# The joint of a convolution and its output projection, run by token block

## What is computed

```python
def conformer_conv(x, w_in, b_in, dw, dw_b, ln_g, ln_b, w_out, b_out):
    h = x @ w_in + b_in
    a, gate = jnp.split(h, 2, axis=-1)
    h = a * jax.nn.sigmoid(gate)
    h = causal_dwconv(h, dw, dw_b)            # 31 taps, per channel
    h = jax.nn.silu(layer_norm(h, ln_g, ln_b))
    return h @ w_out + b_out
```

## Time and profile before

| | us |
|---|---|
| median of three runs | 2142.02 |
| lowest and highest | 2141.66, 2143.29 |
| span of the profiled execution | 2140.8 |
| TensorE busy in it | 2125.7 (99%) |
| VectorE, ACT busy | 1452.6 (68%), 1056.8 (49%) |
| all DMA | 399 MB, mean 186 GB/s |

### The profile page before, as it was taken

One profiled execution on the slowest core, in us unless ns is written; L12 is line 12 of the kernel. 1 busy time (PEld: TensorE's weight loads), 2 busy tenths in 40 slices (PEclk: granted clock), 3 DMA queues, 4 the chain that ended last, 5 costly groups with the idle time before them and its releaser, 6 DMA issues.

```text
span 2140.8 us, 30475 instructions
## 1 busy us (share of the span) xinstructions
PE 2125.7 (99%) x11011; PEld 1812.3 (85%) x11011; DVE 1452.6 (68%) x2137; ACT 1056.8 (49%) x1501; POOL 45.7 (2%) x50
## 2 busy tenths in 40 slices
PE   9999999999999999999999999999999999999998
PEld 7788788888888888888888888888888888888887
DVE  6766757777777774454688867667777777764444
ACT  7554655544445443444554444554544445444443
POOL 5300000000000000000000000000000000000000
PEclk9999999999999999999999999999999999999999
DMA  8555456666666655555656554566666666656553
GB/s 309 175 186 191 138 178 183 190 191 183 194 184 189 191 185 189 193 190 191 191 163 176 181 175 155 191 182 183 190 190 184 194 183 189 192 190 215 195 195 114
DMA packets 513820, 399.07 MB, mean 186 GB/s; under 512 B 6558, under 2 KB 425848, under 8 KB 513408
## 3 DMA queue, kind: packets, MB, share of 16 engines
q1 hardware_dynamic: 513568, 397.96, 60.0%
q10 hardware_dynamic: 192, 0.28, 0.0%
HBM read 396.11 MB, written 2.10 MB: 186 GB/s over the span
## 4 chain that ended last, share of the span: by engine, by line
PE 95%; DVE 2%; DMA 1%; ACT 1%; SPq 0%; issue 0%; DVEq 0%; ACTq 0%
PE acc L1520 35%; PE acc L1525 18%; PE acc L1554 12%; PE acc L1555 12%; PE acc L1556 12%; PE acc L1826 1%; PE acc L1825 1%; PE acc L1824 1%; DMA sb_stage<-in_conv_w_in 1%; DVE sb_w_lo L918 1%; PE aux L1595 0%; PE aux L1835 0%; ACT sb_w_hi L564 0%; PE aux L1783 0%; PE aux L1664 0%
## 5 line engine op out<-in xcount | busy, mean ns | idle before, releaser
L918 DVE TENSOR_TENSOR sb_w_lo<-sb_stage,sb_w_hi 128x1024 fp32r<-128x1024 f32 (+1 forms) x743 | 904.9, 1221 | 516.8 <-ACT sb_w_hi L564 513.4
L564 ACT ACTIVATE sb_w_hi<-sb_stage 128x1024 fp32r<-128x1024 f32 (+1 forms) x743 | 780.4, 1053 | 657.4 <-PE acc L1556 373.9
L1520 PE MATMUL acc<-sb_normed,sb_w_hi 128*128 128x512 f32 x3264 | 1027.6, 396 | 0.0
L1525 PEld LDWEIGHTS acc<-sb_normed,sb_w_lo 128*128 128x128 f32 x3264 | 613.2, 188 | 144.8
L1525 PE MATMUL acc<-sb_normed,sb_w_lo 128*128 128x256 f32 x3264 | 641.4, 278 | 0.0
L1520 PEld LDWEIGHTS acc<-sb_normed,sb_w_hi 128*128 128x128 f32 x3264 | 497.7, 189 | 0.6
L1554 PE MATMUL acc<-sb_w_hi,sb_hidden 128*128 128x512 f32 x674 | 262.5, 389 | 0.0
L1556 PE MATMUL acc<-sb_w_hi,sb_hidden 128*128 128x512 f32 x674 | 262.3, 389 | 0.0
L1555 PE MATMUL acc<-sb_w_lo,sb_hidden 128*128 128x512 f32 x674 | 262.3, 389 | 0.0
L576 ACT ACTIVATE sb_corr<-acc 128x256 f32<-128x256 f32 x204 | 76.8, 376 | 210.8 <-PE acc L1525 210.7
L1556 PEld LDWEIGHTS acc<-sb_w_hi,sb_hidden 128*128 128x128 f32 x674 | 126.5, 188 | 26.4
(11 more groups left out here) (221 smaller groups left out, 1645.1 us busy)
## 6 DMA issues: line engine op xcount, KB each, us to landing
sb_stage<-in_ffn_w_gate SPq DMA_DIRECT2D x86, 1024.0 KB, 5.4
sb_stage<-in_ffn_w_up SPq DMA_DIRECT2D x86, 1024.0 KB, 5.5
sb_stage<-in_ffn_w_down SPq DMA_DIRECT2D x80, 1024.0 KB, 5.0
sb_stage<-in_attn_w_qkv SPq DMA_DIRECT2D x48, 1024.0 KB, 5.3
sb_stage<-in_conv_w_in SPq DMA_DIRECT2D x30, 1024.0 KB, 5.6
sb_stage<-in_conv_w_out SPq DMA_DIRECT2D x16, 1024.0 KB, 5.1
sb_stage<-in_attn_w_o SPq DMA_DIRECT2D x16, 1024.0 KB, 5.0
sb_stage<-in_ffn_w_down SPq DMA_DIRECT2D x8, 768.0 KB, 4.4
```

The costliest lines, as they stand in the source:

```text
L564: nc.scalar.activation(w_hi[:, (2 * first + h) % PIECES, 0:size], stage[:, first % STAGES, off:off + size], ACT.Copy).then_inc(hi_ready, 1)
L918: nc.vector.tensor_tensor(w_lo[:, slot, 0:size], stage[:, first % STAGES, off:off + size], w_hi[:, slot, 0:size].bitcast(F32), ALU.subtrac ...
L1520: nc.tensor.matmul(acc[:, bank, :], w_hi[:, slot, q * P:(q + 1) * P], operand[:, k, :], start=begin, stop=False, skip_group_check=True)
L1525: return nc.tensor.matmul(acc[:, bank, T:2 * T], w_lo[:, slot, q * P:(q + 1) * P], operand[:, k, 0:T], start=False, stop=end, skip_group_c ...
```

## The change

- The two token halves no longer go through the joint together. Statistics, root, scaling, transposes, SiLU and splits of the first four channel tiles are done for the first 128 tokens, then for the other 128 (`ln_moments`, `ln_sqrt`, `ln_invert`, `ln_scale`, `turn_first`, `first_quarter`, `first_split`). TensorE's order is written out in `open_project`: first half through two weight blocks with the second half's inverse and transposes set in between, then the second half through the same two blocks.
- `glu`, `multiply`, `prod_hi`, `prod_lo`, `forward` and `inverse` can be called for one half or one part, and ACT's and VectorE's queues at the joint are set in a new order. The SiLU and root tables are loaded twice each. The dummies are gone.
- The high and low parts of the second `conv_out` block move in both queues; the bias additions come two blocks later.
- In all four chunks `prev_op` is no longer written by ACT and VectorE. `load_prev` on SP copies it with three DMAs out of `glu_op`, the split operand of the first half. For the first three chunks they are issued behind the load of blocks 14, 22 and 30, for the last behind the fifth load of `conv_out`.

The core of the diff:

```diff
+            def load_prev(c):
+                if c:
+                    sp.wait_ge(forward_done, 4 * c)
+                sp.wait_ge(glu_split, TB * c + 1)
+                for at, part in ((0, 0), (32, 1), (64, 0)):
+                    sp.dma_start(prev_op[at:at + 32, :].bitcast(F32), glu_op[P - 32:P, 0, part, :].bitcast(F32)).then_inc(prev_loaded, 16)
...
                     load_in_rows(c)
+                if at % 8 == 6:
+                    load_prev(at // 8 - 1)
             load_dw_bias(CH - 1)
 
             def load_bias():
 
+                load_prev(CH - 1)
                 sp.wait_ge(pieces_done, 2 * B["conv_out"])
...
-                act.wait_ge(glu_ready, TB * c + 1)
-                for at in (0, 64):
-                    nc.scalar.activation(prev_op[at:at + 32, :], value_t[0][P - 32:P, :], ACT.Copy).then_inc(prev_high, 1)
...
-            glu_hi(last)
+            glu_hi(last, [0])
+            for h in range(2):
+                hi(0, (0, B["conv_out"] + 1), h)
+            glu_hi(last, [1])
+            prod_hi(last, 0, [0])
             keep_conv(last - 1, 0, acc)
-            prod_hi(last, 0)
+            prod_hi(last, 0, [1])
             keep_conv(last - 1, 1, acc)
-            prod_hi(last, 1)
-            keep_conv(last, 0, acc, TB)
-            hi(0, (0, B["conv_out"] + 1), 0)
             warm_up(ACT.Sqrt)
...
+            ln_sqrt(0)
+            first_quarter(0, lambda: prod_hi(last, 1, [1]))
+            keep_conv(last, 0, acc, TB)
+            warm_up(ACT.Sqrt)
+            ln_sqrt(1)
+            first_quarter(1)
             keep_conv(last, 1, acc, TB)
-            hi(0, (0, B["conv_out"] + 1), 1)
...
-                if b:
-                    nc.vector.tensor_tensor(prev_op[32:64, :], value_t[0][P - 32:P, :],
-                                            glu_op[P - 32:P, 0, 0, :].bitcast(F32), ALU.subtract).then_inc(prev_split, 1)
...
+            multiply(last, 0, [0])
+            glu_lo(last, 1)
+            multiply(last, 0, [1])
+            prod_lo(last, 0)
+            measure_conv(last - 1, 0)
+            multiply(last, 1, [0])
+            measure_conv(last, 0)
+            ln_moments(0)
+            multiply(last, 1, [1])
+            ln_invert(0)
+            ln_scale(0, 0, 2)
+            prod_lo(last, 1, [0])
+            ln_scale(0, 2, 2)
+            first_split(0, 0)
+            prod_lo(last, 1, [1])
+            for k in range(1, BANKS):
+                first_split(0, k)
+            measure_conv(last - 1, 1)
+            for h in range(2):
+                lo(0, (0, B["conv_out"] + 1), h)
+            measure_conv(last, 1)
+            ln_moments(1)
+            ln_invert(1)
+            ln_scale(1, 0, 2)
+            ln_scale(1, 2, 2)
+            own.done()
+            for k in range(BANKS):
+                first_split(1, k)
...
                     if b:
-                        pe.wait_ge(prev_high, 2 * c + 2)
-                        pe.wait_ge(prev_split, c + 1)
+                        pe.wait_ge(prev_loaded, 48 * (c + 1))
...
-            forward(CH - 1, [0])
-            inverse(CH - 2, acc)
-            forward(CH - 1, [1])
-            inverse(CH - 1, acc, TB)
-            keep_clock(aux[:, 3, 0:P], 9)
+            last = CH - 1
+            forward(last, [0])
+            inverse(last - 1, acc)
+            forward(last, [1], [0])
+            inverse(last, acc, TB, [0])
+            forward(last, [1], [1])
...
+            def open_project():
+                for b in range(TB):
+                    for at in range(2):
+                        c, n = ORDER["conv_out"][at][0], B["conv_out"] + at
+                        bank = (C["conv_out"] + TB * c + b) % BANKS
+                        pe.wait_ge(conv_kept, TB * (CH - 2) + TB * at + b + 1)
+                        for k in range(KB):
+                            h, q = divmod(k, KB // 2)
+                            slot, wide = (2 * n + h) % PIECES, slice(WIDE * q, WIDE * (q + 1))
+                            if (b, at, k) == (0, 0, 2):
+                                inverse(last, acc, TB, [1])
+                            elif (b, at, k) == (0, 1, 1):
+                                turn_first(1)
+                            elif (b, at, k) == (1, 1, 1):
+                                turn_norm(1)
...
+                            if b == TB - 1 and q == 1:
+                                ins.then_inc(pieces_done, 1)
```

More of the change, by code:

```diff
@@ L617, in open_gate, with glu_hi @@
                     nc.scalar.activation(gate_t[b], gate_t[b], ACT.Sigmoid).then_inc(gate_opened, 1)
-            def glu_hi(c):
-                for b in range(TB):
+            def glu_hi(c, rows=range(TB)):
+                for b in rows:
                     act.wait_ge(glu_ready, TB * c + b + 1)
@@ L636, in prod_hi @@
                         act.wait_ge(inverse_done, TB * c)
-                for m in range(2):
+                for m in parts:
                     act.wait_ge(prod_ready, 4 * c + 2 * b + m + 1)
@@ L995, in keep_gate, with glu_value @@
                                                    op1=ALU.add).then_inc(evacuated, 1)
[L997 to L1010, removed]
-                    nc.vector.tensor_tensor(value_t[b], value_t[b], gate_t[b], ALU.mult).then_inc(glu_ready, 1)
-                    if b or c == CH - 1:
-                        glu_lo(c, b)
+            def glu_value(c, b):
+                if c == CH - 1 and b == 0:
+                    dve.wait_ge(rows_done, 1)
+                else:
+                    dve.wait_ge(pieces_done, 2 * (8 * c + 8))
+                nc.vector.scalar_tensor_tensor(out=value_t[b], in0=acc[:, TB + b, :], scalar=row_scale[:, 0, b:b + 1],
+                                               in1=in_rows[:, c % 2, 1, :], op0=ALU.mult,
+                                               op1=ALU.add).then_inc(evacuated, 1)
@@ L1021, in glu_lo, with glu, multiply @@
                 nc.vector.tensor_tensor(glu_op[:, b, 1, :], value_t[b], glu_op[:, b, 0, :].bitcast(F32),
                                         ALU.subtract).then_inc(glu_split, 1)
-            def multiply(c, b):
-                for m in range(2):
+            def glu(c):
+                glu_value(c, 0)
+                glu_gate(c, 0)
+                glu_value(c, 1)
+                glu_lo(c, 0)
+                glu_gate(c, 1)
+                glu_lo(c, 1)
+            def multiply(c, b, parts=range(2)):
+                for m in parts:
@@ L1033, in multiply, with prod_lo @@
                                             ALU.mult).then_inc(prod_ready, 1)
-            def prod_lo(c, b):
-                for m in range(2):
+            def prod_lo(c, b, parts=range(2)):
+                for m in parts:
                     dve.wait_ge(prod_high, 4 * c + 2 * b + m + 1)
@@ L1167, in _ @@
-            own.done()
+            last = CH - 1
+            glu_value(last, 0)
+            glu_gate(last, 0)
+            glu_lo(last, 0)
+            glu_value(last, 1)
+            glu_gate(last, 1)
+            multiply(last, 0, [0])
[7 more added lines that the diff above has]
+            multiply(last, 1, [1])
@@ L1169, in norm_quarter @@
+            ln_scale(1, 2, 2)
+            own.done()
+            for k in range(BANKS):
+                first_split(1, k)
+            for b in range(TB):
+                ln_scale(b, 4, 4)
             def norm_quarter(q):
@@ L1597, in turn_resid, with project @@
                     ins.then_inc(resid_turned, 1)
-            def project(name, operand, tiles, arrivals, between=None, turn=True):
+            def project(name, operand, tiles, arrivals, between=None, turn=True, begin=0):
                 for at, (c, j) in enumerate(ORDER[name]):
+                    if at < begin:
+                        continue
                     before = ENDS[name].get(at - 1) if turn else None
@@ L1666, in triple, with forward @@
                 return nc.tensor.matmul(out, s_lo, m_hi, start=False, stop=end)
-            def forward(c, rows=range(TB)):
+            def forward(c, rows=range(TB), parts=range(2)):
                 if c == 0:
@@ L1685, in forward, with inverse @@
                                (glu_op[:, b, 0, :], glu_op[:, b, 1, :]), b == 0, True).then_inc(forward_done, 1)
-            def inverse(c, banks, at_bank=0):
-                for b in range(TB):
+            def inverse(c, banks, at_bank=0, rows=range(TB)):
+                for b in rows:
                     for m in range(2):
@@ L1756, in up @@
+            turn_first(0)
+            open_project()
+            project("conv_out", conv_op, KD, [(k, OPER["norm"] + BANKS + k + 1) for k in range(BANKS, KD)], next_norm, begin=2)
             def up(name, before):
```

137 lines of the change are left out of this document (76 added, 61 removed).

## The result

The changed kernel takes 2158.39 us (median of 4, 2157.83 to 2160.19) beside 2141.84 us (2141.30 to 2143.29) for the kernel before on the same chip: a ratio of 1.0077, 95% interval 1.0065 to 1.0089, so some 16.5 us slower. The profiled execution spans 2156.3 us, 15.4 more than the 2140.8 of before. It took 2158.07 us, so 1.8 us lie around its span (1.8 to 2.0 in the other runs that show both). By that the profiled execution of before took some 2142.6 us, an estimate, which is above its median and most of what parts 15.4 from 16.5.

The account below looks back on a forecast made before the run. TensorE, busy 99% of a 2140.8 us span, bounds the kernel. 2140.8 + 10.2 (stalls) + 1.6 (clock) − 1.2 (joint) = 2151.4; with 1.2 around the span 2152.6 us, range 2144.5 to 2159.

Parts of the forecast that it names:

- The sign and the place: Whole kernel slower by 0.5%, chance of slower 0.82; TensorE waits on transfers into `prev_op` in blocks 10, 18 and 26.
- the forecast's own span: Kernel time with the forecast's bounds for stalls, clock falls and joint, without rivals: 2147.7 to 2157.7 us, chance 0.73.
- The three stalls: TensorE's first matmul on `prev_op` comes 4.7, 3.1 and 2.4 us later in blocks 10, 18, 26; together 10.2.
- the upper bound of 6.7: Third transfer of each set lands 6.7 us behind the load's issue, as late as `in_rows`; stalls together 12.0 us.
- The reason for the landing: Transfers on SP stand in the queue behind a 1 MB load; the last lands 0.5 us after that load.
- The clock: One fall to half clock, after the first stall in block 10: 1.6 us, 0 to 4.8 possible.
- the term for what lies around the span: Time outside the profiled span of the kernel, 1.2 us, added to 2151.4 (median before 2142.02).
- The joint: Input to output projection: third weight block reached 1.2 us earlier; TensorE idles about 2 us at second half's transposes.
- What was costed at nothing: Joint: extra table loads beyond the SiLU one counted, moved weight splits, later bias additions, fourth set of rows (at most 0.5).
- (a): Rows' transfers do not queue, landing about 2.0 us after issue; delays 1.9 together, kernel 2142.7 us, not slower; chance 0.13.
- (b): Joint gives all 7.5 us back, transfers take 10.2, no fall of the clock: 2144.7 us; chance 0.07.
- (c): Joint loses 1.0, stalls take 12.0, all three bring a fall of the clock (4.8): 2159.8 us; chance 0.07.

Follow-up runs that it names:

- the run with the rows alone: Kernel before with only the first three chunks' previous rows moved by the three transfers, last chunk and joint as before: 2157.85 us, ratio 1.0075.
- ScalarE's queue: Changed kernel with the first three sets of rows issued by ScalarE at the semaphore value of SP's weight load: 2158.27 us, ratio 1.0073.
- The wide matmuls: Changed kernel with 18, 12 and 10 unused matmuls of 512 columns ahead of the waits for rows in blocks 10, 18, 26: 2154.03 us.
- the joint alone: Changed kernel with the previous rows copied and split by ACT and VectorE as before, only the joint's new order kept: 2141.61 us, ratio 0.9999.
- two of these runs, on SP: Changed kernel with rows issued one block earlier, 2142.37 us; or at the same moment but ahead of the 1 MB load, 2144.57 us.
- the mended order: Changed kernel with rows one block earlier, statistics ahead of operand splits, five keep-busy matmuls, second half's transposes one tile later: 2139.08 us, ratio 0.9985.
- the unused matmuls: Changed kernel with result-less matmuls ahead of TensorE's three waits for rows: 128 columns wide 2156.54 us, 512 columns wide 2154.03 us.

## Why the prediction was right, point by point

**The sign and the place: right.** 2152.6 with a range of 2144.5 to 2159 stood against 2158.39. That is above the forecast's own span, which ended at 2157.7; the range, drawn to 2159, holds it by 0.6. TensorE's list of waits names the transfers three times, 3.0 to 5.1 us each, in the blocks forecast, and the run with the rows alone has the whole loss.

**The three stalls: right in sum, 10.9 measured for 10.2.** By block 4.2, 3.5 and 3.2 for 4.7, 3.1 and 2.4, so the sum is in part luck: one block came out below and two above. The issues went as laid out: SP's load at 74.10 for 74.45, and in blocks 18 and 26 by 1.4 us earlier against TensorE's delay, for 1.3. The third landing was put 6.8, 5.9 and 5.6 behind the load's issue; it came 6.6, 6.4 and 6.4 behind. The forecast took the load's own time from each place of the old trace and added 0.5, but with the rows beside it that time no longer varies as it did there; the upper bound of 6.7 was nearer in the last two.

**The reason for the landing: partly wrong.** "They stand in the queue behind a load" described the order on SP. ScalarE's queue gave the same 5.0 us. What matters is that a 1 MB load issued ahead of the rows is still in flight, whatever queue they are on, and the term's size came out right since the nearest row had been measured beside a load too.

**The clock: the mis-sized term, 1.6 forecast and 5.7 measured**, over its own bound of 4.8. The step took one fall for the first stall only, though all three lay between a sparse stretch that had a fall and an idle time of 1.42 that had none. All three had one; the first lasted 6.8 us instead of 3.4 and cost 2.4. The wide matmuls took 5.4 back. With 5.7 in place of 1.6 the same sum gives 2156.7 for 2158.39. Of the 1.7 left, 0.7 are the stalls and the joint, and 0.9 is the term for what lies around the span: its 1.2 set a median against the span of another execution, longer by the estimate above, and 2.1 part the two in the kernel after.

**The joint: 1.1 measured for 1.2, but read against a chance.** (235.0 against 236.3, the two figures behind that term, make 1.3.) The third block came 28.0 us behind the last input matmul (223.90 to 251.92), where before took 29.1. The idle time of about 2 us at the second half's transposes was only 0.63, because the clock fell at 236.1, ahead of it, and the slower matmuls filled it; the forecast had said that such a fall ends in the same idle time, and with the clock up it is 1.99. What it had not weighed is that the old joint's own 1.6 us of half clock does not come in every execution. Between two joints at full clock the gain is 0.4 in the traces, and the times of the joint alone don't settle it.

**What was costed at nothing** stayed so. No weight split shows as a wait behind the joint, and the first matmul on the fourth set moved from 4.92 to 5.18 us behind the last input matmul (212.25 to 229.08 in the traces): 0.3, within the 0.5 allowed.

**The rivals.** (a) The transfers do land in 2.0 us, with nothing else in flight: two of these runs, on SP, are no slower by the 0.2% of the forecast. At the place where the change issues them they don't. The figure of the Trainium skill that stood beside this rival, 2.0 us plus the bytes at 436 GB/s ("DMA: Bandwidth & Descriptors", "Anatomy of one DMA — SWDGE (gpsimd) path"; an estimate of 2.15 us), is stated for DMAs that GpSimd issues; it agrees with their 1.8 to 2.1 us alone (one 2.45) and with SP's 2.0, and not with the 4.3 to 5.6 behind a load. (b) needed the joint to give 7.5; it gave 1.1, and 3.4 with the mended order. (c) had the clock right, a fall behind each stall, but not its worse joint; its 2159.8 was nearer to the time than the forecast, at a chance of 0.07. What came was the forecast's stalls and joint with (c)'s clock.

## What to carry to other kernels

Before an engine's copy is replaced by a DMA, look at what is in flight when the DMA will be issued: the same small transfers were free one block earlier and cost 16 us behind a weight load, and another queue did not help. Moving an issue to another queue also moves what stood behind it, as the load of the biases did here. Price a new stall of TensorE with the half clock behind it. And when a gain is measured from one trace, see whether the old code's loss is there in every execution.

## What was not expected of the hardware

- Much the same idle time is followed by half clock in one place and not in another. Waits of 1.1 and 0.9 us in the old joint led to 3.4 us at half clock before and to none with the rows alone. An idle time of 3.32 us in block 18 led to 3.4 us at half clock in the kernel after, and one of 3.01 us to none with the rows on ScalarE's queue, where one of 2.69 in block 26 of the same execution led to 3.4 us again. TensorE's timeline in that block 18:

```profile
136.27 0.46 PE L1754 MATMUL aux<-sb_prev_op,sb_prev_dft 96*118 96x512 f32 x1 [3.01 <-DMA sb_prev_op<-sb_glu_op]
```

The stretch behind it:

```profile
136.50:140.50 4.00, 4.00 (x19) 3.21 (x19) 0.07 (x1) 0.00 (x0) 0.00 (x0) 1.00 0.84 262
```

- A transfer of 64 KB from SBUF to SBUF lands some 2.0 us after issue alone and 4.3 to 5.6 right behind a 1 MB load, whichever of three queues issues it. An issue of it holds SP for 0.5 to 0.75 us, where a weight load's holds it for 0.37 when no other issue stands just before it; beside the unused matmuls single issues took 1.6 to 1.8.
